# A two-layer hybrid decoder step: tap sets and sample states side by side in the late steps, query blocks of the attention in reverse order

## Time and profile before

| | |
|---|---|
| median of three runs | 1550.04 us |
| the profiled execution | 1550.77 us |
| its span, first to last instruction | 1549.2 us |
| PE busy | 1427.5 us (92% of the span) |
| DVE busy | 794.0 us (51%) |
| ACT busy | 550.9 us (36%) |
| POOL busy | 200.9 us (13%) |
| mean granted TensorE clock | 0.962 of full |
| loop of steps, layer 0 / layer 1 | about 147.1 to 274.7 us / 908.9 to 1035.6 us |

### The profile page before, as it was taken

One profiled execution on the slowest core, in us unless ns is written; L12 is line 12 of the kernel. 1 busy time (PEld: TensorE's weight loads), 2 busy tenths in 40 slices (PEclk: granted clock), 3 DMA queues, 4 the chain that ended last, 5 costly groups with the idle time before them and its releaser, 6 DMA issues. The chain is left out here.

```text
span 1549.2 us, 29026 instructions
## 1 busy us (share of the span) xinstructions
PE 1427.5 (92%) x11720; PEld 1325.7 (86%) x11720; DVE 794.0 (51%) x1623; ACT 550.9 (36%) x907; POOL 200.9 (13%) x134
## 2 busy tenths in 40 slices
PE   4999888997999999999769999899989999999995
PEld 4888765896999999999657977768979999999994
DVE  5489866635444444222346897746264443442224
ACT  3444434534323233222344534264342232222222
POOL 1332233020000000000040422221200000000010
PEclk8999999998999999999879999899989999999997
DMA  6442242221333322233055323312313333323221
GB/s 224 130 133 69 69 108 59 97 85 47 93 93 95 91 85 83 76 93 93 8 202 141 99 69 82 96 58 86 96 55 96 88 88 95 95 63 92 88 70 56
DMA packets 222719, 141.21 MB, mean 91 GB/s; under 512 B 13514, under 2 KB 218674, under 8 KB 222102
## 3 DMA queue, kind: packets, MB, share of 16 engines
q1 hardware_dynamic: 220006, 132.55, 29.2%
q0 software_dynamic: 2624, 7.48, 1.6%
HBM read 124.64 MB, written 11.77 MB: 88 GB/s over the span
## 5 line engine op out<-in xcount | busy, mean ns | idle before, releaser
L1935 DVE TENSOR_TENSOR w_lo<-ring,w_hi 128x1024 fp32r<-128x1024 f32 (+2 forms) x164 | 179.3, 1093 | 399.3 <-ACT w_hi L1322 399.3
L620 PE MATMUL PS<-u_hi,w_hi 128*128 128x260 f32 x1600 | 325.9, 285 | 15.1 <-DVE u_lo L2056 11.4
L1322 ACT CAST w_hi<-ring 128x1024 fp32r<-128x1024 f32 (+2 forms) x168 | 158.9, 946 | 473.4 <-PE PS L620 473.4
L620 PE MATMUL PS<-u_hi,w_lo 128*128 128x260 f32 x1600 | 323.0, 283 | 0.0
L620 PE MATMUL PS<-u_lo,w_hi 128*128 128x260 f32 x1408 | 283.8, 283 | 0.0
L620 PEld LDWEIGHTS PS<-u_hi,w_hi 128*128 128x128 f32 x1600 | 247.1, 189 | 19.1 <-issue 13.5
L620 PEld LDWEIGHTS PS<-u_hi,w_lo 128*128 128x128 f32 x1600 | 248.0, 190 | 0.0
L620 PEld LDWEIGHTS PS<-u_lo,w_hi 128*128 128x128 f32 x1408 | 218.3, 189 | 0.0
L620 PE MATMUL PS<-hid_hi,w_hi 128*128 128x260 f32 x704 | 141.8, 283 | 3.5 <-ACTq L1479 3.5
L620 PE MATMUL PS<-hid_hi,w_lo 128*128 128x260 f32 x704 | 141.8, 283 | 0.0
L620 PE MATMUL PS<-hid_lo,w_hi 128*128 128x260 f32 x704 | 141.4, 282 | 0.0
(11 more groups left out here) (351 smaller groups left out, 2154.5 us busy)
## 6 DMA issues: line engine op xcount, KB each, us to landing
ring<-in_ffn_gate SPq DMA_DIRECT2D x44, 512.0 KB, 3.8
ring<-in_ffn_up SPq DMA_DIRECT2D x44, 512.0 KB, 3.8
ring<-in_w_in SPq DMA_DIRECT2D x36, 512.0 KB, 3.9
ring<-in_ffn_down SPq DMA_DIRECT2D x32, 384.0 KB, 3.4
ring<-in_ffn_down SPq DMA_DIRECT2D x32, 320.0 KB, 3.1
ring<-in_w_out SPq DMA_DIRECT2D x16, 512.0 KB, 4.4
x_store<-x SPq DMA_DIRECT2D x2, 2080.0 KB, 15.7
x<-x_store SPq DMA_DIRECT2D x2, 2080.0 KB, 7.8
```

What stands on the lines that cost most here:

```text
L620: ins = pe.matmul(to[:, h, :], w[:, k - base, :], a[k][:, h * HALF:(h + 1) * HALF], start=(begin and w is whi and a is a_hi), stop=(end an ...
L1322: act.copy(w_hi[part % 2][:, 0:n, :], raw[part % 4][:, 0:n, :]).then_inc(part_hi, 1)
L1935: dve.tensor_tensor(w_lo[part % 2][:, 0:n, :], raw[part % 4][:, 0:n, :], w_hi[part % 2][:, 0:n, :].bitcast(F32), ALU.subtract).then_inc(pa ...
```

## The change

It does six things.

1. The query blocks come in reverse, 3 first (512 keys) and 0 last (128 keys): `STEPS` and the count in the wait on `mixed_out`.
2. The slab order begins 6, 7, 8, 4 in place of 4, 6, 7, 8, so the Sigmoid tiles are tiles 6 and 7 in place of 0 and 1.
3. The pieces of DVE's other work move to earlier steps (3 rounds of `decode_best` in step 0, 5 rounds and the mask in step 1, and so on), PE's and ACT's counterparts with them.
4. The sample states are handled one by one: two each in steps 10 and 11, one each in steps 12 to 15, from sample 4 on all in bank 2. The first product of a sample becomes one tensor_tensor over both halves.
5. The tap sets go to steps 12 to 17 (3, 3, 2, 2, 3, 3), both halves in bank 3; `tap_w` is made by DVE in step 10; SP issues the 32 shifted copies before the load of tile 15. `CS_BANK` is swapped, and `cumulate(0)` waits for the tails to be taken out of bank 2.
6. Before the loop 16 feature matmuls move from between the two key products to before `index_logits`.

```diff
-        CS_BANK = [3, 2, 3, 2]
+        CS_BANK = [2, 3, 2, 3]
-        FEAT_SLABS = [4, 6, 7, 8, 3, 2, 0, 5, 1]
+        FEAT_SLABS = [6, 7, 8, 4, 3, 2, 0, 5, 1]
-        STATES_FROM = 11
+        STATES_AT = {10: (0, 1), 11: (2, 3), 12: (4,), 13: (5,), 14: (6,), 15: (7,)}
-        TAP_SETS = {15: 4, 16: 4, 17: 8}
-        STEPS = [(blk, h) for blk in range(QT) for h in range(HEADS)]
+        TAP_SETS = {12: 3, 13: 3, 14: 2, 15: 2, 16: 3, 17: 3}
+        STEPS = [(blk, h) for blk in reversed(range(QT)) for h in range(HEADS)]
@@ SP, loop over the feature tiles
+                        if f == 15:
+                            sp.wait_ge(gate_in, 2)
+                            sp.wait_ge(tap_edges, 8)
+                            (the 32 copies shifted <- feat, which stood behind the loop)
                         sp.dma_start(raw[(f + 2) % 4], cols("w_in", FEAT0 + s * W + c * P, P))...
@@ PE, before the loop
-                    feature_products(PER_PART)
+                    feature_products(2 * PER_PART)
                     index_logits()
                     key_products(0)
-                    feature_products(PER_PART)
                     key_products(1)
@@ PE
-                    def spread_states(i):
-                        pe.wait_ge(decd_dve, i + 1)
-                        for b in (2 * i, 2 * i + 1):
+                    def spread_states(b):
+                        pe.wait_ge(decd_dve, 1 + b - (b % 2 if b < 4 else 0))
+                        (one sample, bank 2 + b % 2 for b < 4, else bank 2)
...
-                        if j == 10:
-                            turn_state_rows()
...
-                            if h == 0 and blk >= 1:
-                                pe.wait_ge(mixed_out, blk)
+                            if h == 0 and blk < QT - 1:
+                                pe.wait_ge(mixed_out, QT - 1 - blk)
...
+                        if j == 9:
+                            turn_state_rows()
                         feature_products(step_products(j))
-                        if j == 3:
+                        if j == 2:
                             decode_mask()
-                        if j == 6:
+                        if j == 5:
                             decode_prob_turn()
+                        if j == 7:
+                            decode_mix()
                         if j == 8:
-                            decode_mix()
-                        if j == 9:
                             decode_pick()
...
-                    pe.wait_ge(decd_dve, NS // 2 + 1)
+                    pe.wait_ge(decd_dve, NS + 1)
+                    pe.wait_ge(tails_ready, 4)
...
-                    pe.wait_ge(conv_c_done, 1)
                     cumulate(0)
@@ ACT (decode_exp 5 -> 4, sample_mix 9 -> 8, decode_out 10 -> 9, edt's Exp 11 -> 10,
@@      bc_hi 10 -> 9, conv_d_samples_out 6 -> 4)
+                        if j == 15:
+                            conv_c_out(0)
...
-                    conv_c_out(0)
                     conv_c_out(1)
@@ DVE
-                            step(dve.tensor_scalar(prod_n[:, q, c, :], bc[:, c * P:(c + 1) * P], dtx[:, c, b:b + 1], None, ALU.mult))
+                        step(dve.tensor_tensor(prod, bc[:, 0:W].rearrange("p (c n) -> p c n", c=2),
+                                               dtx[:, :, b:b + 1].broadcast_to([P, 2, P]), ALU.mult))
...
+                    def tap_weights():
+                        dve.wait_ge(tap_cols_ready, 17)
+                        dve.wait_ge(dec_pe, 5)
+                        (the tensor_tensor that POOL had)
...
 new order of DVE's other work, step by step:
+ 0 self_scores, decode_best(3)      1 decode_best(5), decode_mask   2 conv_d_samples
+ 3 decode_logits                    4 decode_probs, softplus        5 conv_d(0)
+ 6 decode_columns, conv_d(1)        7 gate_c                        8 conv_d(2)
+ 9 conv_d(3), state_rows           10 tap_weights, states 0 1      11 states 2 3
+12 state 4, conv_d(4)              13 state 5, conv_d(5)           14 state 6, gate_b
+15 state 7, conv_b(0)              behind the loop: conv_b(1)
 the old one:
- 0 self_scores                      1 decode_best(4)                2 decode_best(4), decode_mask
- 3 softplus                         4 decode_logits                 5 decode_probs, conv_d_samples
- 6 conv_d(0)                        7 decode_columns, conv_d(1)     8 gate_c
- 9 conv_d(2)                       10 state_rows, conv_d(3)        11 states 0 1, conv_d(4)
-12 states 2 3, conv_d(5)           13 states 4 5, gate_b           14 states 6 7
-15 conv_b(0)                        behind the loop: conv_b(1)
@@ POOL
-                        if f == 15:
-                            tap_weights()
```

More of the change, by code:

```diff
@@ L941, in _ @@
                         feature_products(step_products(j))
-                        if STATES_FROM <= j < STATES_FROM + NS // 2:
-                            spread_states(j - STATES_FROM)
+                        for b in STATES_AT.get(j, ()):
+                            spread_states(b)
                         if j >= 3 and j % 2:
@@ L1313, in conv_c_out @@
                         act.wait_ge(conv_c_summed, c + 1)
-                        act.activation(feat[:, GG + c, 0:SEQ], bank(3 - c), ACT.Identity, bias=pcol("cconv_b", c))\
+                        act.activation(feat[:, GG + c, 0:SEQ], bank(3), ACT.Identity, bias=pcol("cconv_b", c))\
                            .then_inc(conv_c_done, 1)
@@ L1836, in sample_states @@
                         settle()
-                        dve.wait_ge(decd_pe, 2 * i + 3)
-                        two = [(q, 2 * i + q, bank(2 + q), c) for q in range(2) for c in range(2)]
-                        for q, b, bc, c in two:
-                            step(dve.tensor_scalar(prod_n[:, q, c, :], bc[:, c * P:(c + 1) * P], dtx[:, c, b:b + 1], None, ALU.mult))
+                        dve.wait_ge(decd_pe, b + 2)
+                        bc = bank(2 + b % 2 if b < 4 else 2)
+                        prod = prod_n[:, b % 2]
@@ L1841, in sample_states @@
+                        step(dve.tensor_tensor(prod, bc[:, 0:W].rearrange("p (c n) -> p c n", c=2),
+                                               dtx[:, :, b:b + 1].broadcast_to([P, 2, P]), ALU.mult))
                         settle()
-                        for q, b, bc, c in two:
+                        for c in range(2):
                             h = ssm[:, 2 * b + c, :]
-                            step(dve.scalar_tensor_tensor(h, h, edt[:, 0, c, b:b + 1], prod_n[:, q, c, :], ALU.mult, ALU.add))
+                            step(dve.scalar_tensor_tensor(h, h, edt[:, 0, c, b:b + 1], prod[:, c, :], ALU.mult, ALU.add))
@@ L1845, in sample_states @@
                         settle()
-                        for q, b, bc, c in two:
-                            step(dve.tensor_tensor_reduce(prod_n[:, q, c, :], ssm[:, 2 * b + c, :], bc[:, W + c * P:W + (c + 1) * P],
-                                                          1.0, 0.0, ALU.mult, ALU.add, y_dec[:, c, b:b + 1]))
-                        settle()
-                        dve.sem_inc(decd_dve, 1)
-                        if i == NS // 2 - 1:
-                            dve.sem_inc(ssm_done, 1)
+                        for c in range(2):
+                            last = dve.tensor_tensor_reduce(prod[:, c, :], ssm[:, 2 * b + c, :], bc[:, W + c * P:W + (c + 1) * P],
+                                                            1.0, 0.0, ALU.mult, ALU.add, y_dec[:, c, b:b + 1])
+                            if c == 0:
+                                step(last)
@@ new lines, in sample_states @@
+                        last.then_inc(decd_dve, 1)
+                        if b == NS - 1:
+                            dve.wait_ge(decd_dve, NS + 1)
+                            dve.sem_inc(ssm_done, 1)
+                    def tap_weights():
+                        dve.wait_ge(tap_cols_ready, 17)
+                        dve.wait_ge(dec_pe, 5)
+                        n = 2 * 4 * TAP_GROUPS
+                        dve.tensor_tensor(tap_w.rearrange("p c b g m -> p (c b g) m"),
+                                          const("tap_mask").unsqueeze(1).broadcast_to([P, n, 32]),
+                                          tap_col.rearrange("p c b g -> p (c b g)").unsqueeze(2).broadcast_to([P, n, 32]),
+                                          ALU.mult).then_inc(tap_w_ready, 1)
@@ L1888, in _ @@
                             self_scores()
+                            dve.wait_ge(dec_dve, 1)
+                            decode_best(3)
                         elif j == 1:
[L1890 to L1891 removed]
+                            decode_best(5)
+                            decode_mask()
                         elif j == 2:
[L1893 to L1894 removed]
+                            conv_d_samples()
                         elif j == 3:
+                            decode_logits()
+                        elif j == 4:
+                            decode_probs()
```

(11 more changed lines are left out.)

85 lines of the change are left out of this document (30 added, 55 removed).

## The result

| | before | after |
|---|---|---|
| median, five runs each | 1550.04 us | 1559.06 us (1557.73 to 1559.45) |
| ratio after / before | | 1.0056, 95% interval 1.0041 to 1.007 |
| the profiled execution | 1550.77 us | 1558.77 us |
| its span | 1549.2 us | 1557.2 us |
| mean granted clock | 0.962 | 0.961 |

A forecast was written before the change was run, and what follows sets the result against it. PE, 92% busy, bounds the kernel, losing time only to waits and low clock. Waits +5.0 us in layer 0 and +7.7 in layer 1, clock -3.7, total +9.0 on 1550.0: 1559.0 us; own range 1553.2 to 1567, overall 1542 to 1568.

The forecast's parts named there:

- (a): Step 0: 512-key softmax and search rounds on DVE put PE's first transposes at 156.0, before 153.41; wait 2.6 us.
- (b): Step 1: five search rounds and the mask on DVE put the transposes at 162.35, PE there at 161.5; wait 0.85 us.
- (e): `decode_exp` comes only after tile 7, DVE idle since 174; step 5's transposes at 186.3; PE waits 0.6 us.
- (f): Samples' Silu now in step 4, so step 5's Exp needs a table load; wait for tile 8 1.9 us, was 0.3.
- (c): Tile 6: ACT does step 2's Exp, cast and Sigmoid table load first; out at 165.7; wait 2.8 us, was 1.58.
- (d): Tile 7 ends step 3, Sigmoid again, with nothing behind it to cover; wait 3.2 us, was 0.68.
- (g): Tile 9 ends step 6 with nothing behind it; wait 1.85 us, was 1.04.
- Late sum: PE's waits from tile 10 on: 7.25 us against 12.5 and 9.8; saves 5.2 in layer 0, 2.5 in layer 1.
- clock term: Of 7.3 us lost to low clock in both layers, about half was to come back: -3.7 us.
- Edits at nothing: Parts priced at no net time: split tap sets and sample states, `tap_w` on DVE, SP's copies (cover 19 us), moved products.
- The late cover wins: Rival: DVE's and ACT's chains in steps 0 to 5 run ahead of PE; early cost some 3 us a layer; 1541; chance 0.22.
- Dearer switches: Rival: four table switches on PE's path each cost another 1.28 us as a gap; 10 on top, 1569; chance 0.03.

The follow-up runs named there:

- e8: The changed kernel plus 20 and 24 matmuls nobody reads, in PE's waits at tiles 6 and 7; ratio to the kernel before 1.0025.
- e1: The kernel before with only the new slab order (6, 7, 8, 4 first); ratio to the kernel before 1.0088.
- e5: The changed kernel with the query blocks in forward order again; ratio to the kernel before 1.0071.
- e4: The changed kernel with the old slab order (4, 6, 7, 8), softplus and the samples' Silu placed to suit; ratio to the kernel before 0.9971.
- e9: e7 with POOL's split of tile 7 held back until DVE has normalised step 0; ratio to the kernel before 0.9928.
- e7: e4 with the samples' search spread over steps 0 to 2 and softplus in step 3; ratio to the kernel before 0.9953.

## Why the prediction was right, and where two errors cancelled

- **(a) start of step 0:** right for DVE: 156.0 forecast, 156.13 measured. The wait was 3.92 and not 2.6, because PE arrived 1.2 us earlier than I counted (at 152.2, and not 153.4).
- **(b), (e), (f):** I forecast waits of 0.85, 0.6 and 1.9 us. None is there. DVE did stand idle in step 4 as said; its timeline has

```profile
183.34 0.17 DVE L1772 RECIPROCAL side<-side 128x2 f32<-128x2 f32 x1 [6.22 <-ACT side L1288]
```

  But PE came later too, at half clock. e8 brought (e) and (f) back as 0.72 and 0.25. The sum counted PE's arrival at full clock all through; that is the step that failed. It accounts for (e), but of the 1.9 of (f) only 0.25 came back, so that term was too large besides; (b) came back in no run.
- **(c), (d), (g):** forecast 2.8, 3.2 and 1.85; measured 2.67, 3.10 and 1.69. Tile 6 resumed at 166.56 in place of 165.7.
- **Early sum:** 3.92 + 2.67 + 3.10 + 1.69 = 11.4 measured where 13.8 were forecast, so +7.8 and not +10.2 a layer.
- **Late sum:** 7.25 forecast, 1.36 + 1.69 + 2.19 + 1.30 = 6.5 measured. The waits for DVE went as said. Waits together: +12.7 forecast, (17.9 - 16.1) + (17.8 - 13.4) = +6.2 measured.
- **The clock term was mis-sized, in sign too:** I let the loss fall by half, by 3.7 us. It rose, by the count above from 8.4 to 13.6: +5.2. The late loss vanished as I said, but each of the three early waits of 2.7 to 3.9 us brought a fall of its own. They cost 1.7, 1.7 and 3.4 us (the two stretches from 178.58 on). Rows 4 and 5 had losses behind waits of 1.3 to 5.04, so new waits of about 3 us should have been priced with a fall each and not with half of the old loss, though not as certain: in e1 and e5 three such waits had none.
- **Together:** +6.2 + 5.2 = 11.4, somewhat over the 4.4 + 5.3 = 9.7 us by which the loops grew. One reason is that low clock while PE waits is counted twice: the third fall had begun at about 180.0, and PE resumed at 180.95. The span grew by 8.0 only; 1.5 us were won back between the two loops. So the waits were put 6.5 us too high and the clock 8.9 too low, and that these nearly cancel is luck. Had the waits been sized as they were and the clock kept at -3.7, the forecast would have been 1552.5, 6.5 us under the median. Nor does the sum's own range, 1553.2 to 1567, follow from its 7 to 12 us a layer: with -3.7 for the clock these give 1552.6 to 1562.6.
- **Edits at nothing:** SP's 32 copies took 22.2 us as forecast (22.6), but started at 204.19 and not near 193, so that 11 of the 19 us of cover were used. The queue of SP in the kernel after:

```profile
204.19 11.17 SPq L553 DMA_DIRECT2D arena<-hid  x16
215.40 2.50 SPq L553 DMA_DIRECT2D side<-hid  x4
217.94 8.47 SPq L553 DMA_DIRECT2D arena<-hid  x12
```

  PE has no wait for the taps. `tap_w` on DVE took 2.28 us against 2.8 forecast. The last tap set ended at 279.21, forecast near 277.
- **Rivals.** "The late cover wins" asked for an early cost under 7.5 us a layer with the clock fully back: the early waits cost 7.8, and the clock wasn't back. e4 is that rival's kernel: late cover without Sigmoid among the Exps, and it is faster. Dearer switches: none. The activations at 165.91 and 182.21 start within 0.02 us of the end of their loads. The Trainium skill, "ScalarE: Activation LUTs", section "What ACT_TABLE_LOAD costs", has a drain of about 1.38 us beside the load; these rows show none. What a Sigmoid tile among the Exps cost was 1.42 us more of wait at each of two tiles (e1), 1.28 of it the load, and clock on top; the other two of the four switches, for `decode_exp` and for the Exp of step 5, show no wait of PE of their own.

## What to carry to other kernels

On an engine that is busy 92% of the span, price a new wait as its length plus a possible fall of the clock behind it, and give both ends. In the kernel after, each wait of 2.7 us or more had one, of 1.7 or 3.4 us; at tile 6 of e1 and e5 waits of 3.0 had none in three of four cases. Don't stack later waits on an arrival at full clock. Keep activations of another table out of the steps in which a matmul bank waits for ACT; where several edits come in one change, undo the one that adds a wait first. A step that reads like idle cover (POOL's split beside DVE's normalising) can be the longest thing on the path: compare the longest and the median duration of the same instruction.

## What the runs showed of the hardware that I had not expected

- The length of a wait did not tell whether the clock would fall. The start wait of 1.99 us was followed by a clock of 0.72 over 6 us (e9, layer 0; pairs of products 0.64 us in place of 0.40), while in layer 1 of the same run one of 1.9 us was followed by 1.00. In the kernel before the wait of 1.3 us for DVE was followed by half clock in layer 1 (matmuls from 989.21 on the earlier trace rows) and by 1.00 in layer 0. In e1 the wait of 3.00 us was followed by 1.00 in layer 0 and by a fall in layer 1.
- Unread matmuls, 44 of them in two waits of each layer, made the kernel 0.31% faster.
- POOL's subtraction stretched DVE's normalising of 512 columns from 0.49 to 1.95 us (e7) and a DVE instruction of 8 x 8 elements from 0.15 to 2.29 (e5), but not the rounds of maximum and match-replace beside it: in the kernel after, POOL's split ran from 151.71 to 154.06, and DVE's rounds kept the 0.42 and 0.40 us they take elsewhere. DVE's timeline there:

```profile
152.80 0.42 DVE L1744 MAX8 side<-side 8x8 f32<-8x257 f32 x1
...
153.33 0.40 DVE L1746 MATCH_REPLACE8 side<-side 8x257 f32<-8x257 f32 x1
```
